# Where a transformer kernel renormalises between two matrix products: another order on three engines, and sums of squares by column groups

## The reference

```
x = x + g1 * rmsnorm(y, norm_g[i, 1])            # y: output of the mixer
h = rmsnorm(x, norm_g[i, 2]) * (1.0 + sc2) + sh2
y = jnp.square(jax.nn.relu(h @ ffn_w1[i])) @ ffn_w2[i]
x = x + g2 * rmsnorm(y, norm_g[i, 3])
```

## Time and profile before

| | |
|---|---|
| median of 3 runs | 2215.14 us (2204.17 to 2215.4) |
| the profiled execution, its own time | 2212.78 us |
| its span in the profile | 2211.0 us |
| PE busy | 2128.2 us, 96% |
| DVE, ACT, POOL busy | 1226.6, 824.8, 93.5 us |
| mean granted PE clock | 0.978 |

### The profile page before, as it was taken

How to read it: one execution, slowest core, us unless ns; L and a number is a source line. 1 busy time by engine, 2 the same in 40 slices (tenths; PEclk the granted TensorE clock), 3 DMA queues, 4 the chain that set the end, 5 groups by cost and what they waited for, 6 DMA issues and landing times.

```text
span 2211.0 us, 29777 instructions
## 1 busy us (share of the span) xinstructions
PE 2128.2 (96%) x11614; PEld 1781.0 (81%) x11614; DVE 1226.6 (55%) x1994; ACT 824.8 (37%) x1229; POOL 93.5 (4%) x71
## 2 busy tenths in 40 slices
PE   7999899999998999999999999999999999999997
PEld 5898788888888998888888888886666688888886
DVE  4567677666667445556333336426557756535455
ACT  3333344324234322335243343335445534324243
POOL 0000010000001003301000000100000000000000
PEclk8999989999999999999999999899999999999998
DMA  9452224666551433231222222222012131222221
GB/s 295 153 191 77 78 77 157 197 210 200 187 190 58 155 95 113 77 115 39 95 95 95 96 95 91 63 69 86 1 48 80 46 115 58 95 96 95 97 84 67
DMA packets 224630, 239.34 MB, mean 108 GB/s; under 512 B 6642, under 2 KB 219021, under 8 KB 223877
## 3 DMA queue, kind: packets, MB, share of 16 engines
q1 hardware_dynamic: 182757, 193.73, 27.0%
q10 hardware_dynamic: 41760, 44.06, 6.0%
HBM read 230.81 MB, written 6.31 MB: 107 GB/s over the span
## 4 chain that ended last, share of the span: by engine, by line
PE 67%; issue 18%; DVE 6%; ACT 3%; DMA 3%; DVEq 1%; POOL 1%; SPq 1%; ACTq 0%; POOLq 0%
PE bank L546 43%; PE bank L1150 4%; PE bank L686 2%; PE bank L740 2%; PE bank L1098 1%; DMA ada_raw<-in_ada_w 1%; PE bank L1087 1%; PE bank L1045 1%; PE bank L644 1%; PE bank L1075 1%; DVE ada_acc L1753 1%; PE bank L1133 1%; PE bank L1121 1%; POOL rstd L2572 1%; ACT w_hi L1218 1%
## 5 line engine op out<-in xcount | busy, mean ns | idle before, releaser
L1742 DVE TENSOR_TENSOR w_lo<-raw,w_hi 128x2048 fp32r<-128x2048 f32 x137 | 314.0, 2292 | 232.7 <-ACT w_hi L1218 232.5
L546 PE MATMUL bank<-h_hi,w_hi 128*128 128x512 f32 x1040 | 407.7, 392 | 0.0
L546 PE MATMUL bank<-h_hi,w_lo 128*128 128x512 f32 x1040 | 405.5, 390 | 0.0
L546 PE MATMUL bank<-h_lo,w_hi 128*128 128x512 f32 x1040 | 405.4, 390 | 0.0
L1218 ACT ACTIVATE w_hi<-raw 128x2048 fp32r<-128x2048 f32 x147 | 280.1, 1906 | 306.0 <-PE bank L546 302.2
L546 PE MATMUL bank<-g_hi,w_hi 128*128 128x512 f32 x688 | 271.6, 395 | 7.9 <-DVE g_lo L2531 5.0
L546 PE MATMUL bank<-g_hi,w_lo 128*128 128x512 f32 x688 | 269.5, 392 | 0.0
L546 PE MATMUL bank<-g_lo,w_hi 128*128 128x512 f32 x688 | 269.3, 391 | 0.0
L546 PEld LDWEIGHTS bank<-h_hi,w_lo 128*128 128x128 f32 x1040 | 195.6, 188 | 40.9
L546 PEld LDWEIGHTS bank<-h_lo,w_hi 128*128 128x128 f32 x1040 | 195.7, 188 | 40.3 <-issue 0.2
L546 PEld LDWEIGHTS bank<-h_hi,w_hi 128*128 128x128 f32 x1040 | 195.6, 188 | 40.2 <-issue 0.2
(11 more groups left out here) (422 smaller groups left out, 3702.5 us busy)
## 6 DMA issues: line engine op xcount, KB each, us to landing
raw<-in_ffn_w SPq DMA_DIRECT2D x64, 1024.0 KB, 5.3
ada_raw<-in_ada_w ACTq DMA_DIRECT2D x40, 1024.0 KB, 5.2
raw<-in_w_up SPq DMA_DIRECT2D x22, 1024.0 KB, 5.0
raw<-in_b_w_in SPq DMA_DIRECT2D x16, 1024.0 KB, 5.3
raw<-in_w_in SPq DMA_DIRECT2D x15, 1024.0 KB, 5.7
raw<-in_a_w_in SPq DMA_DIRECT2D x12, 1024.0 KB, 5.4
ada_head<-in_ada_w SPq DMA_DIRECT2D x8, 1024.0 KB, 12.1
raw<-in_b_w_out SPq DMA_DIRECT2D x8, 1024.0 KB, 5.2
```

What stands on the lines that cost most here:

```text
L546: mm = pe.matmul(o, x, y, start=(k == 0 and j == 0), stop=(k == kc - 1 and j == 2))
L1742: dve.tensor_tensor(w_lo[s][:], raw[s][:], f32(w_hi[s][:]), ALU.subtract).then_inc(sem("split_done"), 1)
```

## The change

All five boundaries are written anew on PE, DVE, ACT and POOL; what they compute is the same.

- The first half of the next product runs with k outside: for each k all four output blocks (12 products), in banks 0 to 3. Half 1 keeps its order and uses banks 4 to 7. In `ffn0` the same is done with token chunks.
- PE's `sums` takes the squares of y of the last block straight from ACT's tile as a second summand (4 one-column products), so that DVE's last `y_sum` goes. `sums` and `spread_half` stand earlier.
- The column sums of the squares of x: `x_rows` multiplies ones (32 columns) by each of the 8 blocks of squares (256 columns), the blocks spread over four groups of 32 columns of the array; ACT copies the 128 x 256 result to SBUF (`x_row`), and `x_turn` sums it with 2 one-column products. Each column sum is then 32 times too big, and `variance` divides by 32 \* D.
- DVE merges two blocks at a time (two L1847 operations, one drain, one addition of 128 x 512); POOL adds nothing any more. ACT squares two blocks at a time.
- On DVE the second piece of `rest_of` for the second tile comes after the merges of half 0, and `variance`, `diagonal` and the merges no longer have a piece of `rest_of` between them. Merges of half 1 stand between the steps of h of half 0, and the split of tile t+2 comes after h of half 1, in one piece. On ACT `w_split` of that tile moves ahead of h.

```diff
+            def sums(name, half):
+                kb_, o = BOUNDS[name], bank[norm_banks(name, half)[0]]
+                for i, sq in enumerate([sqa, T[3]]):
+                    if i == 0:
+                        pe.wait_ge(sem(f"sq_ready{half}"), 6 * kb_ + 1)
+                    else:
+                        pe.wait_ge(sem("y_squared"), 12 * kb_ + 8 + 4 * half)
+                    for c in range(2):
+                        mm = pe.matmul(o[:, c:c + 1], sq[:, half * HALF + c * P:half * HALF + c * P + P],
+                                       ones[:, 0:1], start=(i == c == 0), stop=(i == c == 1), skip_group_check=True)
+                mm.then_inc(sem(f"sq_used{half}"), 1)
+            def x_rows(name, half, first):
+                kb_, o = BOUNDS[name], bank[norm_banks(name, half)[2]]
+                for i in (0, 1) if first else (2, 3):
+                    pe.wait_ge(sem(f"sq_ready{half}"), 6 * kb_ + i + 2)
+                    for b in (2 * i, 2 * i + 1):
+                        r = slice(32 * (b % 4), 32 * (b % 4) + 32)
+                        mm = pe.matmul(o[r, 0:HALF], ones[:, 0:32], xsq[:, b], start=first, stop=not first)
+                if not first:
+                    mm.then_inc(sem(f"x_rows{half}"), 1)
+            def x_turn(name, half):
+                kb_, o = BOUNDS[name], bank[norm_banks(name, half)[2]]
+                pe.wait_ge(sem(f"sq_ready{half}"), 6 * kb_ + 6)
                 for c in range(2):
+                    mm = pe.matmul(o[:, c:c + 1], xsq[:, 0, c * P:c * P + P], ones[:, 0:1], start=True, stop=True)
                 mm.then_inc(sem(f"sq_used{half}"), 1)
...
                         for k in range(KB):
-                            if (half, m, k) == (1, 0, 5):
-                                sums(0, 9 * kb_, sqa)
-                            if (half, m, k) == (1, 1, 2):
-                                spread_half(0, 2 * kb_)
-                            if two and (half, m, k) == (1, 3, 2):
-                                x_sums(name, 0, range(4, KB))
+                            if (half, m, k) == (1, 0, 3):
+                                sums(name, 0)
+                            if (half, m, k) == (1, 0, 7):
+                                spread_half(name, 0)
+                            if two and (half, m, k) == (1, 2, 2):
+                                x_rows(name, 0, True)
+                            if two and (half, m, k) == (1, 3, 0):
+                                x_rows(name, 0, False)
+                            if two and (half, m, k) == (1, 3, 3):
+                                x_turn(name, 0)
                             if two and (half, m, k) == (1, 3, 7):
...
-                        if two and (half, m) == (1, 2):
-                            x_sums(name, 0, range(4))
...
+            def norm_step(name, k):
+                if k == 1:
+                    sums(name, 1)
+                if k == 2:
+                    spread_half(name, 1)
+                if k == 5:
+                    x_rows(name, 1, True)
+                if k == 6:
+                    x_rows(name, 1, False)
+                if k == 7:
+                    x_turn(name, 1)
+                if k == KB:
+                    spread_half(name, 1, True)
...
+                for k in range(KB):
+                    norm_step(name, k)
+                    pe.wait_ge(sem("h_ready0"), 8 * BOUNDS[name] + k + 1)
+                    for m in range(4):
+                        step(0, m // 2, m % 2, k, bank[m], True)
...
                 if two:
-                    x_squares(0)
-                    for m in range(3):
-                        y_square(m, y[m], hs[1])
-                    hi(0, range(3))
+                    for i in range(4):
+                        x_squares(0, i)
+                    y_square(0, y[0], hs[1])
+                    x_row(0)
+                    y_square(1, y[1], hs[1])
+                    w_split(u + 1, 0, 4 * q + 2)
+                    y_square(2, y[2], hs[1])
+                    hi(0, range(2))
                     y_square(3, y[3], hs[1])
...
+                def merge(half, i):
+                    t = TT[i % 2]
+                    for b in range(2):
+                        dve.scalar_tensor_tensor(t[:, b, hs[half]], Y[:, 2 * i + b, hs[half]], y_gain_[:, 2 * i + b:2 * i + b + 1],
+                                                 bank[norm_banks(name, half)[1]][:, 0:HALF], ALU.mult, ALU.mult)
+                    dve.drain()
+                    x = X[:, 2 * i:2 * i + 2, hs[half]]
+                    dve.tensor_tensor(x, x, t[:, :, hs[half]], ALU.add).then_inc(sem(f"x_ready{half}"), 1)
...
+                def first_half():
+                    variance(0)
+                    if two:
+                        diagonal(0)
+                        spread_done(0)
+                        for i in range(4):
+                            merge(0, i)
+                        y_out(1, 0)
+                        y_out(1, 1)
+                rest_of(t2, 1, next_w[name][1], 2, first_half)
...
                 if two:
                     y_sum(1, 0)
+                    variance(0, True)
+                    y_out(1, 2)
+                    diagonal(0, True)
                     y_sum(1, 1)
+                    spread_done(0, True)
+                    h_scale(0, 0)
+                    h_scale(0, 1)
+                    h_rest(0, 0)
+                    y_out(1, 3)
+                    h_rest(0, 1)
+                    h_scale(0, 2)
                     y_sum(1, 2)
+                    h_rest(0, 2)
+                    h_scale(0, 3)
+                    variance(1)
+                    h_rest(0, 3)
+                    h_scale(0, 4)
+                    diagonal(1)
+                    h_rest(0, 4)
+                    spread_done(1)
+                    merge(1, 0)
+                    merge(1, 1)
+                    h_scale(0, 5)
+                    h_rest(0, 5)
+                    merge(1, 2)
+                    merge(1, 3)
+                    h_scale(0, 6)
+                    h_scale(0, 7)
+                    h_rest(0, 6)
+                    h_rest(0, 7)
+                    variance(1, True)
+                    diagonal(1, True)
+                    spread_done(1, True)
...
                 h_parts(1, range(KB))
+                if two:
+                    rest_of(t2 + 2, 0, (w_hi[0], w_lo[0]), 1)
                 rest_of(t2 + 2, 1, (w_hi[1], w_lo[1]), 1)
```

More of the change, by code:

```diff
@@ L604, in sums @@
                 mm.then_inc(sem(f"sq_used{half}"), 1)
[L606 to L613, removed]
@@ new lines, in step @@
+                    wh, wl = (w[:, k * 256 + b * P:k * 256 + b * P + P] for w in next_w[name][s])
+                    for j, (x, y) in enumerate([(wh, h_hi[:, k, hs]), (wh, h_lo[:, k, hs]), (wl, h_hi[:, k, hs])]):
+                        mm = pe.matmul(o[:, hs], x, y, start=(k == 0 and j == 0), stop=(k == KB - 1 and j == 2))
+                    if k == KB - 1 and last:
+                        mm.then_inc(sem("block_done" if half else "half_done"), 1)
+                for s in range(2):
+                    pe.wait_ge(sem("split_done"), t + s + 1)
@@ new lines, in first_pair @@
+                for m in range(4):
+                    evacuated(m, q)
+                if name == "out2":
+                    for half in range(2):
+                        for s in range(2):
+                            for k in range(KB):
+                                if (half, s, k) == (0, 0, 4):
+                                    sums(name, 1)
+                                if (half, s, k) == (0, 1, 2):
+                                    spread_half(name, 1)
+                                if s == 0:
+                                    pe.wait_ge(sem(f"h_ready{half}"), 8 * BOUNDS[name] + k + 1)
+                                for b in range(2):
+                                    step(half, s, b, k, bank[2 * s + b], half == 1)
+                    return
@@ L1889, in boundary @@
+                rest_of(t2, 1, next_w[name][1], 2, first_half)
+                if not two:
+                    diagonal(0)
+                    spread_done(0)
                 if two:
-                    merge(0, range(KB))
-                    for m in range(3):
-                        y_out(1, m)
                     y_sum(1, 0)
+                    variance(0, True)
+                    y_out(1, 2)
+                    diagonal(0, True)
                     y_sum(1, 1)
-                    variance(0, 9 * kb_ + 9, 1)
@@ L1896, in boundary @@
-                    y_sum(1, 2)
-                    diagonal(0, 2 * kb_ + 1)
-                    spread_done(0, 2 * kb_ + 1)
-                    h_parts(0, range(KB), {2: lambda: y_out(1, 3), 3: lambda: y_sum(1, 3),
-                                           5: lambda: variance(1, 9 * kb_ + 1), 6: lambda: diagonal(1, 2 * kb_)})
-                    spread_done(1, 2 * kb_)
-                    merge(1, range(KB))
```

(1 more changed line is left out.)

217 lines of the change are left out of this document (91 added, 126 removed).

## The result

The changed kernel takes 2191.24 us (median of 6 runs, 2187.91 to 2192.96), the kernel before 2208.85 us on the same chip (6 runs, 2202.2 to 2215.4). The ratio is 0.991, 95% interval 0.9892 to 0.9928. The profiled execution took 2191.51 us, its span is 2189.7 us, 21.3 less than before. On one of the chips a single run of the kernel before took 2765.18 us at a mean granted clock of 0.714; it is a slow one, and medians and ratios here go by the fast ones.

The account below looks back on a forecast made before the run. PE bounds the kernel (2128 of 2211 us busy). Four boundaries gave -13.1 us, out2 -0.4, the clock -4.5: together -18.0 from the profiled 2212.8, so 2195 us; forecast 2187 to 2202 (0.62), range with rivals 2184 to 2208.

Parts of the forecast that it names:

- Step 1: At b_out, `sums` waits only for ACT's square, not DVE's last addition: variance at 983.24, not 983.91, -0.67 us.
- Step 2: At b_out, POOL's power takes 0.70 us, not 1.62, with no `rest_of` piece there: -0.92 us, diagonal at 984.20.
- Step 3: At b_out, half 0's merges by pairs, 1.55 us each: four take 6.21 us, not 7.14, ending at 991.6, -2.5 us.
- Step 4: At b_out, ACT's squares of pairs take 0.63 us each: the last ends at 992.36, not 994.69.
- Step 5: At b_out, x sums take 1.85 us a half, not 3.4, but ACT's copy and a turn join the chain.
- Step 6: Next product's half 0 at b_out: PE waits 0.75, 1.33 and 0.5 us; last half at 1019.4, not 1022.8, -3.3 us.
- Step 7: At b_out, last half keeps 96 products; next tile at 1031.3, not 1034.6; moved work hidden by 1.8 us or more.
- Four boundaries at 3.3: Sum over the four two-norm boundaries, each 3.3 us shorter by the b_out ledger: -13.1 us.
- The clock: Low clock at the boundaries costs 7.0 us; 2.5 remain after the change: -4.5 us; bounds -7.0 and +11.
- seven low stretches of eight: Slower rival: PE throttled twice per boundary, 4.4 us each, 2227 us; passes 0.5% at seven stretches of eight; chance 0.04.
- the groups do share the array: Opposite of a rival: column groups run one after another, 0.35 us each, 1.7 us a boundary, 2201 us; chance 0.10.
- the chain got shorter: Opposite of a rival: pair merges cost 1.75 us, POOL's power stays 1.6, boundary gains under 1 us, 2206 us; chance 0.12.

Follow-up runs that it names:

- fourth_sum_on_vector: Changed kernel with the fourth block's squares added by VectorE again in both halves of all five boundaries; 2197.2 us, ratio 0.9921 to the kernel before.
- wide_sums: Kernel before with the x sums' products by 64 columns of ones instead of 1, same number and order; 2204.68 us, ratio 0.998 to the kernel before.
- changed_again: The changed kernel itself, repeated unaltered as a control beside the other kernels; 2191.72 us, ratio 0.9917 to the kernel before.
- k_outside_alone: Kernel before with only k outside in the next product's first half at a_out, b_out and ffn1; 2207.85 us, ratio 0.999 to the kernel before.
- columns_half1: Changed kernel with half 1's x sums back to 16 one-column products; 2181.52 us, ratio 0.9861 to the kernel before; repeated, 2186.86 us.

## Why the prediction was right, point by point

The first product of half 1 in b_out stands at 980.55 before and 969.83 after; with the 10.73 us between them taken off, the ledger's times and those of the profile after are:

| | ledger | measured |
|---|---|---|
| first variance | 972.51 | 972.59 |
| first diagonal | 973.47 | 973.57 |
| end of the merges of half 0 | 980.87 | 980.99 |
| second spread of half 0 | 985.47 | 985.51 |
| first product of h | 987.87 | 987.94 |
| second spread of half 1 | 1006.27 | 1006.20 |
| last half | 1008.67 | 1008.53 |
| next tile | 1020.57 | 1020.54 |

- Step 1: right; fourth_sum_on_vector gives 1.7 us for both halves of it.
- Step 2: right, and shown: 0.70 us without the piece, 0.92 more with it.
- Step 3: the pair takes 1.55 us as worked out from its parts (974.78 to 976.34 is one); undone it costs 1.9 us a boundary.
- Step 4: ACT's last square runs from 981.10 for 0.63 us; the ledger's end, shifted, is 981.63. Right. Squares by pairs and ACT's new order were not undone by themselves.
- Step 5: a call of `x_rows` advances PE by 0.63 and 0.75 us in half 0 of b_out, against 0.7. The column groups are worth 1.27 us in half 0, bound by the chain as the step said. That in half 1, where PE waits anyhow, the longer chain costs more than the shorter products save (0.4 to 0.8 us) follows from the step's own words ("ACT's copy (0.38) and a turn stand in the chain now"), and I drew it only for half 0.
- Step 6: PE waits 0.52 and 0.92 us for the last squares and 0.30 for h, where 0.75, 1.33 and 0.5 were worked out; right in kind, nearly half as large again as measured or more, and of no weight, as the last half shows.
- Step 7 and the moved work: the last half took 12.0 us at full clock, and no wait for a bank, a weight tile or a split shows behind it. Right there. But 115 us behind a_out PE waits 0.92 us for DVE's `ada_acc` (at 450.28) where the kernel before doesn't; whether the work moved behind the boundary brings that on stays open.
- "Four boundaries at 3.3": right in the sum. What the old order takes at full clock is shown by wide_sums, which is that order at the same speed (in b_out its starts agree with those of the kernel before to 0.1 us up to 36.9 us behind the first product) with less low clock. Its ffn1 is at full clock throughout (PE alone, from the first product to the next tile):

```profile
1349.60:1402.30 52.70, 47.09 (x370) 1.00 0.20 61
```

Its other three have one low stretch each, in a last half that then takes 13.1 us, and less 1.1 us they take 54.1, 54.4 and 53.8 us. The new order takes 51.0 (a_out, less 1.1), 50.8, 50.7 and 49.0. So the order gave 3.1, 3.6, 3.1 and 3.7 us, 13.4 in place of 13.1. out2 gave 0.2, not 0.4.
- The clock: this is the term that was too small. The same lengths say that the clock cost the kernel before 2.5, 0.6, 2.5 and 3.0 us, 8.6 in its profile. The prediction had 7.0, because it took one length, b_out's 51.7 from `sums` on, for all four; ffn1 at full clock is over 1 us shorter than b_out in both orders. And 1.1 us remained in the changed kernel, 2.2 in changed_again (two stretches), where 2.5 were left. The profiles gave 7.5 us where 4.5 were taken, nearly all of the 3.3 by which the profiled execution came out below 2194.8.
- How much of that is luck: the profiled execution of the kernel before was slower than its median by 3.9 us, that of the changed kernel by 0.3. Between the medians the change is worth 17.6 us, where 18.0 were forecast, and with 13.6 for the order some 4 are left for the clock (an estimate from these two numbers).
- A slip in the recorded rivals: seven low stretches of eight would make it 10.3 us slower (7 x 4.4 - 7 - 13.5), which is 0.47%, just under the 0.5% named.
- Of the rivals, the groups do share the array; the chain got shorter; the clock fell once or twice for 3.4 us and never ahead of all last halves. The calls of `x_rows` took about the 0.7 us of the sum. So the rule of the Trainium skill, "TensorEngine Tiling (Array Packing)", Key Properties, on draining at a change of mode shows here as no more than the 0.3 us a call charged for. The advice to loop k-contiguously, so that PE stays warm, stands in the Trainium skill, "TensorE: Matmul & The Clock Gate", in the section "HAM oscillation — how this bites in real kernels", not in the one that the prediction names. It is given there for loops that wait for a DMA between steps of k, and k outside is not that loop, so it decides little here: of the 8.6 us, 7.5 and 6.4 came back in the two profiles, with shorter waits and fewer one-column records.

## What to carry to other kernels

k outside alone was worth nothing that the times could tell, all the rest without it a loss, and both together 18 us: undo each part alone before judging either. Ask of each half of a pipelined stage what binds it; column groups, which save matrix time at the price of a copy, gained 1.3 us in one half and lost 0.4 to 0.8 in the other, where PE waited anyhow. And a ledger in program order, with durations from one trace, met a new order to 0.15 us over 50 us; it should be made for each place that it is multiplied by, not for one, and checked against a kernel without low clock before the clock's share is read off.

## What was not expected of the hardware

The program reaches its first boundary at very different times in the same code, and it goes with the clock. Windows of the kernel before and of k_outside_alone (PE's columns only), the first 276 us:

```profile
0.00:276.00 276.00, 246.83 (x1560) 0.92 0.49 159
```

```profile
0.00:276.00 276.00, 245.72 (x1639) 0.97 0.51 163
```

In these 276 us PE is idle for 29 and 30 us, so waits don't make the difference; the first reached half 1 of a_out at 286.2 us, the second at 276.6. Over all fourteen profiles: a clock of 0.97 gives 276.6 and 277.4, 0.94 gives 281.8 to 284.4, 0.92 and 0.93 give 284.4 to 286.2. That is up to 9.6 us between executions, half of this change's effect and most of the 13 us over which the runs of the kernel before spread. columns_half1 was at 277.4 in its first profile and 281.8 in its second, the changed kernel at 283.3 and 286.2. Its unprofiled runs have no trace, but the mean clock of each run is on record: 0.989 to 0.993 in the four of columns_half1, 0.986 to 0.988 in the five of its repeat, 0.985 to 0.989 in the twelve of the changed kernel. Over the 23 runs of the kernel before 0.001 of mean clock goes with 1.5 us, so some 5 of the 10 us by which the first median lies under the changed kernel are the clock's (an estimate from these numbers). The rest, like the 4 us of the repeat, is hardly clear of the intervals, and some 2 us of it would be the 0.4 to 0.8 us a boundary found above. Boundaries read from the trace separate changes of 1 us that medians don't.

A product of 64 columns in this type takes the time of one of 1 column (272 against 245 ns mean, 0.106 us from start to start in both), and with 64 columns the granted clock fell less (0.986 against 0.981 over the program, in wide_sums and the kernel before).
